# Order of a step's work on ScalarE and VectorE in a software-pipelined latent attention: transposed probabilities before or after the next head's queries and keys

## The reference, cut to what matters

```python
q = (rms_norm_2(c_q, q_norm_g) @ w_uq).reshape(B, S, 8, 64 + 32)      # S = 512
q_rope = apply_rope(q[..., 64:], cos, sin)
kv = (rms_norm_2(c_kv, kv_norm_g) @ w_ukv).reshape(B, S, 8, 64 + 64)
k_nope, v = kv[..., :64], kv[..., 64:]
# per block of 128 queries and per head: causal softmax over 512 keys
s = q_nope @ k_nope^T + q_rope @ k_rope^T      # scaled by 96 ** -0.5
p = softmax(where(mask, s, neg))
o = p @ v
```

## Time and profile before

| | us |
|---|---|
| median of the runs (3) | 2760.99 |
| lowest, highest | 2760.68, 2764.58 |
| the profiled execution, its own time | 2771.13 |
| its span in the profile | 2769.3 |
| TensorE busy in the span | 2688.4 |
| VectorE busy | 1455.1 |
| ScalarE busy | 942.9 |
| first scores of the latent attention | at 2062.3 |
| first matmul of the merge behind it | at 2191.2 |

### The profile page before, as it was taken

How to read it: one execution, slowest core, us unless ns; L and a number is a source line. 1 busy time by engine, 2 the same in 40 slices (tenths; PEclk the granted TensorE clock), 3 DMA queues, 4 the chain that set the end, 5 groups by cost and what they waited for, 6 DMA issues and landing times.

```text
span 2769.3 us, 33070 instructions
## 1 busy us (share of the span) xinstructions
PE 2688.4 (97%) x12126; PEld 2206.7 (80%) x12126; DVE 1455.1 (53%) x1706; ACT 942.9 (34%) x1361; POOL 402.0 (15%) x324
## 2 busy tenths in 40 slices
PE   6999999999999999999999999999998899899998
PEld 5888888888888888888888888877777787788887
DVE  5444346664443454434666444338886476542443
ACT  3222224332222332222433222234656334241332
POOL 3000111220001100002122000115643121200002
PEclk8999999999999999999999999999998799899999
DMA  5333332233333233333323333352331133133332
GB/s 130 95 95 94 97 76 83 68 99 98 92 95 96 84 106 98 97 90 79 94 59 92 101 96 95 91 102 63 84 69 35 50 92 99 46 107 97 93 99 76
DMA packets 521450, 243.06 MB, mean 88 GB/s; under 512 B 73488, under 2 KB 517904, under 8 KB 521360
## 3 DMA queue, kind: packets, MB, share of 16 engines
q1 hardware_dynamic: 509808, 241.82, 31.3%
q10 hardware_dynamic: 11552, 0.05, 0.2%
HBM read 239.74 MB, written 2.10 MB: 87 GB/s over the span
## 4 chain that ended last, share of the span: by engine, by line
PE 84%; DVE 10%; ACT 3%; issue 1%; POOL 1%; ACTq 1%; POOLq 0%; DVEq 0%
PE bank L617 12%; PE bank L618 12%; PE bank L619 12%; PE psT L617 9%; PE psT L618 9%; PE psT L619 9%; PE psS L617 3%; PE psS L618 3%; PE psS L619 3%; DVE wlo L1481 2%; POOL zc L2087 1%; ACT sc L1182 1%; ACT whi L1109 1%; DVE sc L1616 1%; DVE psT L1771 1%
## 5 line engine op out<-in xcount | busy, mean ns | idle before, releaser
L1481 DVE TENSOR_TENSOR wlo<-raw,whi 128x1024 fp32r<-128x1024 f32 x466 | 627.8, 1349 | 511.2 <-ACT whi L1109 486.5
L617 PE MATMUL bank<-xhi,whi 128*128 128x512 f32 x1776 | 703.6, 396 | 31.6 <-DVE xlo L1509 21.4
L618 PE MATMUL bank<-xlo,whi 128*128 128x512 f32 x1776 | 694.7, 391 | 0.0
L619 PE MATMUL bank<-xhi,wlo 128*128 128x512 f32 x1776 | 694.7, 391 | 0.0
L1109 ACT ACTIVATE whi<-raw 128x1024 fp32r<-128x1024 f32 x463 | 484.5, 1048 | 335.4 <-PE psT L619 330.7
L617 PEld LDWEIGHTS bank<-xhi,whi 128*128 128x128 f32 x1776 | 335.3, 189 | 107.5 <-DVE xlo L1509 22.6
L618 PEld LDWEIGHTS bank<-xlo,whi 128*128 128x128 f32 x1776 | 335.5, 189 | 71.2 <-issue 2.9
L619 PEld LDWEIGHTS bank<-xhi,wlo 128*128 128x128 f32 x1776 | 334.9, 189 | 70.6
L619 PE MATMUL psT<-hhi,wlo 128*128 128x512 f32 x704 | 278.4, 395 | 0.0
L617 PE MATMUL psT<-hhi,whi 128*128 128x512 f32 x704 | 278.4, 395 | 0.0
L618 PE MATMUL psT<-hlo,whi 128*128 128x512 f32 x704 | 278.3, 395 | 0.0
(11 more groups left out here) (403 smaller groups left out, 3619.0 us busy)
## 6 DMA issues: line engine op xcount, KB each, us to landing
raw<-in_ffn_wg SPq DMA_DIRECT2D x88, 512.0 KB
raw<-in_ffn_wu SPq DMA_DIRECT2D x88, 512.0 KB
raw<-in_ffn_wd SPq DMA_DIRECT2D x64, 512.0 KB
raw<-in_w_mlp SPq DMA_DIRECT2D x64, 512.0 KB
raw<-in_w_in SPq DMA_DIRECT2D x53, 512.0 KB
raw<-in_ffn_wd SPq DMA_DIRECT2D x32, 384.0 KB
raw<-in_w_in SPq DMA_DIRECT2D x24, 256.0 KB
raw<-in_w_out SPq DMA_DIRECT2D x11, 512.0 KB
```

The source lines that it names most:

```text
L617: pe.matmul(dest, a, rhs_hi(k), start=start and k == 0, stop=False)
L618: pe.matmul(dest, a, rhs_lo(k), start=False, stop=False)
L619: mm = pe.matmul(dest, b_, rhs_hi(k), start=False, stop=stop and k == tiles - 1)
L1481: dve.tensor_tensor(wlo[:, a:a + UNIT], raw[:, a:a + UNIT], whi[:, a:a + UNIT].bitcast(F32), ALU.subtract).then_inc(s_split, 1)
```

## The change

In ScalarE's and in VectorE's list of a step, the block that makes the high or low part of the transposed probabilities of step `s-1` now stands ahead of `head`, and no longer between `head` and `head_q`. Nothing is added or removed. In odd steps and in step 0 the order is as it was, since `head` or the block is not there.

```diff
@@ ScalarE
-                if s % 2 == 0 and s // 2 + 1 < H2:
-                    head(s // 2 + 1)
                 if 1 <= s <= MLA_STEPS:
                     act.wait_ge(b_tt, s)
                     act.activation(pt2h[:, :], psT[:, 0:(TB + 1) * P], ACT.Copy).then_inc(b_th, 1)
+                if s % 2 == 0 and s // 2 + 1 < H2:
+                    head(s // 2 + 1)
                 if s % 2 == 0 and s // 2 + 1 < H2:
                     head_q(s // 2 + 1)
```

## The result

The changed kernel took 2780.11 us (median of 4 runs, 2779.55 to 2781.41), the kernel before 2762.78 us (4 runs, 2760.68 to 2766.38): ratio 1.006, 95% interval 1.0047 to 1.0074, or 13 to 20 us. Timed again beside 29 runs of the kernel before (2767.34 us, 2760.99 to 2771.88) the changed one took 2778.88 us: ratio 1.0041, 1.0028 to 1.0054, or 8 to 15 us. The changed kernel repeats within 3 us, the one before spreads over 11. The forecast was +14.4 us, which lies inside both intervals; its absolute figure, 2775.4 us, is 4.7 and 3.5 us under the two medians.

A forecast was written before the change was run, and what follows sets the result against it. The prediction took the order of small steps, with waits in it, to bound the latent attention loop. Path +9.7 us and clock +4.7 us gave +14.4 us on 2761.0 us: 2775.4 us, range 2763.5 to 2782 us.

The forecast's parts named there:

- The weight split loses its cover: Steps 2, 6, 10, 12: split now waits for the transposes, delaying `q2l`, exponentials and next scores, +2.40 us each.
- The gain is swallowed: Step 12's pair: products with the values start 0.45 us earlier, but TensorE then waits for the later exponentials.
- Step 4 is covered by the sums: TensorE's layer norm column sums after step 4's transposes outlast the exponentials' delay; -0.1 us, ends -0.44 and 0.
- Step 8 gains 2.25 us that are worth nothing: Step 8's products start 2.25 us earlier, but exponentials hold step 10's scores; +0.2 us, ends 0 and +0.6.
- The path: Sum over the six changed steps of the loop, without the clock: 4 x 2.40 - 0.1 + 0.2 = +9.7 us.
- The clock: Longer TensorE idles in steps 3, 7, 11, 13 lower its clock; +4.7 us, ends 0 and +5.6.
- Its main term: Stretch from step 4's scores to its transposes, at full clock before, loses 3.8 us to a low clock.
- The other one: Stretch from step 14's scores: clock falls at its start, not only in its second half, about 0.9 us more.
- the rival of an idle in step 9: More than 15.3 us: an idle in step 5 or 9 too, or clock back later; up to 2782 us; chance 0.10.
- The profiled execution lies 10 us over the median, for both kernels: Profiled run assumed 10 us over the median in both kernels: 2785.5 us profiled, 2775.4 us median.
- Behind the loop nothing absorbs it: After the loop TensorE goes straight into the merge, waiting for the loop's last output, so the delay counts.

The follow-up runs named there:

- two split runs: Changed kernel with the weight split alone put back ahead: 2775.12 us; kernel before with the split alone moved behind the transposed probabilities: 2773.87 us.
- the run with the probabilities before the keys: Kernel before with `pt2h` and `pt2l` moved ahead of `k2h` and `k2l` only: 2767.98 us, ratio 1.0009.
- maxima-first run: Kernel before with `k2l`, `q2l`, layer norm mean behind odd steps' maxima, `pt2h` and `pt2l` ahead of keys, `chi` and `clo` one step later: 2759.50 us, ratio 0.9975.
- squares later: The maxima-first run with the layer norm's four squares one step later on ScalarE: 2762.34 us, ratio 0.9984.

## Why the prediction was right, step by step

- **The weight split loses its cover.** Right, by the row: ScalarE idle 4.76 us ahead of `pt2h`, then `whi`, then the queries. Worked out: `q2l` 2.40 us later against the transposes; measured 2.42. The scores: +2.40 forecast, +2.45 in four pairs. The two split runs add what the prediction's words pass over, though its sum had it: only 1.3 us of this is the split, and 1.1 us are the bank reads that also moved behind the probabilities.
- **The gain is swallowed.** Right: shown by the run with the probabilities before the keys, where the gain stood alone.
- **Step 4 is covered by the sums.** Right: no wait for exponentials before scores 6, and T4 to T6 is +0.1 us (-0.1 forecast).
- **Step 8 gains 2.25 us that are worth nothing.** Right in kind: TensorE's wait for `pt2l` went from 2.77 to 0.56 us there, and T8 to scores 10 is +0.4 us (+0.2 forecast). `wlo` took 1.48 us beside GpSimd's work (at 2137.19) and not 1.23, which the upper end had allowed for.
- **The path**: +9.7 us forecast, +10.3 us measured.
- **The clock**: +4.7 us forecast, +3.2 us by the two profiles. Its main term was exact (scores 4 to T4 +3.7 us, 3.8 forecast). The other one was not: from scores 14 on I expected +0.9 us, and it was -0.6 us; the clock was low from the start of that stretch, as expected, but came back for a while in step 15 (1.00 from 2191 to 2193), where before it stayed at 0.50 from 2170 to 2196. Steps 10 and 12, +0.8 and -1.0 us, cancelled. Before scores 10 there was a fifth wait for exponentials, 2.50 us, which the sum had not named (the rival of an idle in step 9 had). That waits of some 3.6 us would bring the low clock was my estimate, from two waits of 1.93 and 2.77 us with the clock at 0.50 some 2 us and 1 us after their ends. The changed profile bears it out: around each of the four waits of 3.65 and 4.79 us the clock fell to 0.50, between some 2.6 us before the scores that follow the wait and 0.6 us after their start. Two stretches got shorter behind longer waits all the same: scores 12 to T12 by 1.0 us (wait of 0.44 us before, 3.65 changed), scores 14 to the merge by 0.6 us (0.79 and 3.65). And the transposes of steps 4, 8 and 12 show a return of the clock in two cases only: during the projections of steps 8 and 12 it rose from 0.50 to 1.00 (by 2125 and 2159), while from 2086.83 to 2093.70 it stood at 1.00 throughout.
- **The profiled execution lies 10 us over the median, for both kernels.** This failed. The changed kernel's profiled execution is its median (2779.58 and 2780.11 us); that of before is 8 us over its own. So 2785.5 us was forecast for the profile and 2779.6 measured. Behind the loop the profile of before is 5.3 us longer than the changed one, at 0.72 and 0.82 in the cross attention's window; why, isn't shown.
- **Behind the loop nothing absorbs it.** True for the work, not for the clock: behind the loop (clock 0.82 in the cross attention's window, 0.72 before, 0.75 in most others) the changed kernel was 5.3 us shorter than the one profile of before, and 3 us shorter than most of the other kernels, in both of its profiles. I can't say how much of that belongs to the change.
- **How good the hit is.** In the loop +14.4 us stand against +13.5, and the order of the terms is right. That 14.4 us also lies between the two differences of the medians, 17.3 and 11.5 us, is in part luck. The spans differ by only 8.1 us, and no profile shows what a median execution of the kernel before looks like inside. The 2761.0 us on which the absolute figure was built came from three runs; the median of 29 later ones is 2767.3 us.

## What to carry to other kernels

When an item is moved ahead of another in an engine's list, look at what the other did while it waited: here a weight split that needed nothing stood in front of a wait, and the new order put the wait in front of it. Then ask which of the two consumers ends the period: a value that is 0.45 us earlier for one is worth nothing while another, queued behind, sets the next turn. The cheap gain was elsewhere, some 7 us in the maxima-first run: put behind the item that the next wait hangs on everything that is needed later than it.

## What the runs showed of the hardware

- TensorE's clock added a second cost to this schedule's waits. The same work (scores 4 to T4, scores 12 to T12), 6.9 us at clock 1.00, took 9.7 to 10.9 us at mean clocks of 0.57 to 0.66 behind waits for exponentials of 1.4 to 3.7 us (the changed kernel, the two split runs and, in step 4, the one with the probabilities before the keys). A schedule that was 4.3 us ahead at scores 12 was no faster as a whole, and matmuls whose results nobody reads, put into the waits, took it from 0.9984 to 0.9949 of the kernel before.
- The wait's length alone didn't decide here. Before scores 12 of the changed kernel TensorE waited 3.65 us, as before scores 4, and the first matmul there took 0.30 us and not 0.44: the clock fell to 0.50 only at 2163, 0.6 us after the scores' start, where in step 4 it had fallen at 2088, 1.4 us before it. Nor did the last wait alone: in the kernel before the stretch from scores 12 took 10.67 us behind a wait of 0.44 us and began at 0.50, to which the clock had fallen by 2149, while the one from scores 4 took 6.87 us at 1.00 behind 0.79 us.
- With filler matmuls in the waits the two stretches that had taken 10.6 us (changed kernel, scores 4 to T4, clock 0.59) and 10.4 us (squares later, scores 12 to T12, clock 0.60) took 6.4 and 7.2 us, both at 1.00.
